# Second block's gated scan: the running maxima of all steps ahead of the scan, latent steps overlapped, two weightings on ScalarE, rows spread by a broadcast stationary operand

## The reference

```python
b = jnp.cumsum(lfc, axis=-1)
logd = jnp.where(mask, b[..., :, None] - b[..., None, :] + lic[..., None, :], -jnp.inf)
inter = b + m[..., None]
m_s = jnp.maximum(inter, jnp.max(logd, axis=-1))
dmat = jnp.exp(logd - m_s[..., None])
s = jnp.einsum('bhsd,bhrd->bhsr', qc, kc) * dmat
w_inter = jnp.exp(inter - m_s)
num = jnp.einsum('bhsr,bhrd->bhsd', s, vc) + w_inter[..., None] * jnp.einsum('bhvk,bhsk->bhsv', C, qc)
den = jnp.sum(s, axis=-1) + w_inter * jnp.einsum('bhk,bhsk->bhs', n, qc)
h = num / jnp.maximum(jnp.abs(den), jnp.exp(-m_s))[..., None]
log_w = b[..., -1:] - b + lic
m_new = jnp.maximum(b[..., -1] + m, jnp.max(log_w, axis=-1))
w = jnp.exp(log_w - m_new[..., None])
decay = jnp.exp(b[..., -1] + m - m_new)
C_new = decay[..., None, None] * C + jnp.einsum('bhr,bhrv,bhrk->bhvk', w, vc, kc)
```

## Time and profile before

| | us |
|---|---|
| median of 3 runs (4122.18 to 4126.77) | 4125.26 |
| the profiled execution | 4122.54 |
| its span in the trace | 4120.8 |
| first constant's DMA of the stage issued | at 2356.07 |
| last state update of the scan over | at 2546.65 |
| first DMA of the next stage issued | at 2691.06 |

### The profile page before, as it was taken

How to read it: one execution, slowest core, us unless ns; L and a number is a source line. 1 busy time by engine, 2 the same in 40 slices (tenths; PEclk the granted TensorE clock), 3 DMA queues, 4 the chain that set the end, 5 groups by cost and what they waited for, 6 DMA issues and landing times. The chain is left out here.

```text
span 4120.8 us, 37527 instructions
## 1 busy us (share of the span) xinstructions
PE 3426.4 (83%) x11876; PEld 1539.3 (37%) x11877; DVE 1973.6 (48%) x4086; ACT 659.6 (16%) x1532; POOL 932.9 (23%) x811
## 2 busy tenths in 40 slices
PE   7988998587899979999869845778788788888876
PEld 3345443332233323333335434544333233333332
DVE  5834223422333232232244055656666767667676
ACT  1011121000000000000022111412222222222212
POOL 2000000102222221021220040003444444444443
PEclk9999999699999989999989966899999999999998
DMA  9825333469999995597972000038999999999997
GB/s 333 284 87 200 137 115 114 188 229 408 376 364 366 364 412 233 215 363 283 385 262 98 27 0 0 1 150 345 421 415 412 421 408 408 422 403 422 417 421 327
DMA packets 194149, 1157.36 MB, mean 281 GB/s; under 512 B 25659, under 2 KB 27995, under 8 KB 74356
## 3 DMA queue, kind: packets, MB, share of 16 engines
q1 hardware_dynamic: 97140, 565.17, 35.3%
q0 software_dynamic: 80576, 564.05, 33.5%
q10 hardware_dynamic: 16320, 26.75, 2.1%
HBM read 1128.96 MB, written 48.68 MB: 286 GB/s over the span
## 5 line engine op out<-in xcount | busy, mean ns | idle before, releaser
L2462 DVE SCALAR_TENSOR_TENSOR mod<-q_uv,mix 128x1024 f32<-128x1024 f32 x512 | 627.1, 1225 | 391.5 <-DMA q_uv<-in_peer_uv,q_picks 387.0
L1149 PE MATMUL ps<-wt,e_xT 128*64 128x512 f32 x3200 | 729.4, 609 | 97.7 <-DMA wt<-in_w_exp 96.9
L2167 POOL DMA_INDIRECT q_uv<-in_peer_uv,q_picks x512 | 569.5, 1112 | 1053.9 <-PE ps L2259 720.8
L2259 PE MATMUL ps<-q_uv,q_dg 128*128 128x512 f32 x1024 | 518.7, 663 | 144.5 <-ACT q_dg L2336 144.5
L2259 PE MATMUL ps<-q_uv,tri 128*128 128x512 f32 x1024 | 465.4, 608 | 81.3 <-ACT tri L2336 81.3
L1129 POOL COPY wt<-e_land 128x2048 f32<-128x2048 f32 x124 | 237.7, 1917 | 1019.4 <-DMA e_land<-in_w_exp 1019.4
L1149 PEld LDWEIGHTS ps<-wt,e_xT 128*64 128x64 f32 x3200 | 236.9, 140 | 580.5 <-issue 430.0
L2259 PEld LDWEIGHTS ps<-q_uv,q_dg 128*128 128x128 f32 x1024 | 213.1, 213 | 441.1 <-issue 441.1
L1149 PE MATMUL ps<-wt,e_aT 128*64 128x512 f32 x1600 | 356.0, 597 | 21.5 <-ACT e_aT L1202 21.5
L2259 PEld LDWEIGHTS ps<-q_uv,tri 128*128 128x128 f32 x1024 | 194.9, 194 | 348.0 <-issue 347.9
L454 PE MATMUL ps<-hT,wt 128*128 128x512 f32 x640 | 285.1, 602 | 1.5 <-DVE wt L781 1.5
(11 more groups left out here) (439 smaller groups left out, 3402.7 us busy)
## 6 DMA issues: line engine op xcount, KB each, us to landing
wt<-in_w_exp SPq DMA_DIRECT2D x260, 1024.0 KB, 17.5
e_land<-in_w_exp SPq DMA_DIRECT2D x124, 1024.0 KB, 24.4
wt<-in_w_in_units SPq DMA_DIRECT2D x15, 2048.0 KB, 11.1
mod<-in_w_mod_units SPq DMA_DIRECT2D x48, 512.0 KB, 5.8
scratch_xs<-const_zeros SPq DMA_DIRECT2D x8, 2080.0 KB, 9.4
mod<-in_w_ada_units SPq DMA_DIRECT2D x32, 512.0 KB, 7.5
p_ring<-in_w_in SPq DMA_DIRECT2D x7, 2048.0 KB, 10.6
e_xg<-scratch_xs ACTq DMA_DIRECT2D x104, 128.0 KB, 7.3
```

What stands on the lines that cost most here:

```text
L1149: ins = nc.tensor.matmul(ps[64 * h:64 * h + 64, at, :], lhs[:, k % 4, 64 * (k // 4):64 * (k // 4) + 64], wt[:, u, a, h * W:(h + 1) * W], s ...
L2167: pool.indirect_dma_start(out=uv[:, n % NR, :, :].rearrange("p a d -> p (a d)"), out_offset=None, in_=A["peer_uv"], in_offset=bass.Indirec ...
L2259: last = nc.tensor.matmul(acc(t)[:, c, :], dg(n), uv[:, n % NR, 1, c * W:(c + 1) * W], start=fresh, stop=closing)
L2462: dve.scalar_tensor_tensor(junk[:, n % 2, :], uv[:, n % NR, 0, :], 1.0, mix[:, tile_of(k), :], ALU.mult, ALU.mult, accum_out=ap[:, k % 2, ...
```

## The change

It leaves GpSimd's work, the attention and every other stage as they were. In the scan:

- SyncE loads the gates' bias first, with a semaphore of its own (`s_bg`), and VectorE waits for it alone. The gate arrays are laid out direction first, so that the prefix sums take 3 products instead of 18.
- The sum of squares for the attention comes ahead of the scan.
- A first phase computes spreads and maxima for all six steps into arrays with an entry for each step (`mx`, `mr`, `ms`, `ek`, `eq`). A row is spread by using a column of `aa`, read with step 0 as a 128 x 128 stationary operand, against the identity (`spreads`), in banks 2 and 3 or 0 and 1 by turns. The logs of the latent steps are kept, one in `lgd` and three in the memory of `sq` (`logs`). The two context steps' states are made between the spreads. A second phase runs the four latent steps.
- ScalarE weights the keys (`weighted`, 8 instructions instead of VectorE's 2) and scales the state's product (8 instead of VectorE's 8). The first state is copied, not added to zeros, and the last one isn't made. `kw` has two buffers, in the memory of `qT`.
- TensorE's order in a latent step is: state's product, transposes, weighted keys by values, decayed products by values, then the next step's query-key products. VectorE divides a step's output after it has prepared the next one, and takes the statistics (`bn_stats`) as outputs become final.

```diff
@@ TensorE
+                def spreads(i):
+                    if i >= 2:
+                        pe.wait_ge(s_ar, i - 1)
+                    for u in range(8):
+                        last = nc.tensor.matmul(spread(i)[:, u // 4, (u % 4) * P:(u % 4 + 1) * P],
+                                                aa[:, i, u:u + 1].broadcast_to([P, P]), ident[:, :], start=True, stop=True)
+                    last.then_inc(s_ab, 1)
...
+                def states(i):
+                    pe.wait_ge(s_kw, i + 1)
+                    for u, (d, hh) in enumerate(units()):
+                        last = nc.tensor.matmul(sums_at(u, 5), kw[:, i % 2, u, :], va[:, steps[i][d], hh, :], start=True, stop=True)
+                    last.then_inc(s_kv, 1)
...
+                pe.wait_ge(s_aa, 1)
+                spreads(0)
+                spreads(1)
+                spreads(2)
+                states(0)
+                spreads(3)
+                pe.wait_ge(s_C, 1)
+                states(1)
+                spreads(4)
+                spreads(5)
+                pe.wait_ge(s_ar, NSTEP)
+                products(NTC)
+                for i in range(NTC, NSTEP):
+                    c = i - NTC
+                    pe.wait_ge(s_C, i)
+                    for u, (d, hh) in enumerate(units()):
+                        t = steps[i][d]
+                        last = nc.tensor.matmul(sums_at(u, 5), ct[:, hh, t * P:(t + 1) * P], CT[:, u, :], start=True, stop=True)
+                    last.then_inc(s_nm, 1)
+                    pe.wait_ge(s_s, c + 1)
+                    for u in range(8):
+                        last = nc.tensor.transpose(ps[:, u // 4, (u % 4) * P:(u % 4 + 1) * P], logs(c)[:, u, :], ident[:, :])
+                    last.then_inc(s_st, 1)
+                    if i + 1 < NSTEP:
+                        pe.wait_ge(s_ns, c + 1)
+                        states(i)
+                    pe.wait_ge(s_sT, c + 1)
+                    if c >= 1:
+                        pe.wait_ge(s_na, c)
+                    for u, (d, hh) in enumerate(units()):
+                        last = nc.tensor.matmul(sums_at(u, 2), sT[:, u, :], va[:, steps[i][d], hh, :], start=True, stop=True)
+                    last.then_inc(s_nm, 1)
+                    if i + 1 < NSTEP:
+                        products(i + 1)
@@ ScalarE
+                def weighted(i):
+                    if i >= 2:
+                        act.wait_ge(s_kv, i - 1)
+                    for u, (d, hh) in enumerate(units()):
+                        last = act.activation(kw[:, i % 2, u, :], kt[:, steps[i][d], hh, :], ACT.Copy, scale=ek[:, 0, i, u:u + 1])
+                    last.then_inc(s_kw, 1)
...
+                for c in range(NT):
+                    i = NTC + c
+                    act.wait_ge(s_nm, 2 * c + 1)
+                    if c >= 2:
+                        act.wait_ge(s_fin, c - 1)
+                    for u in range(8):
+                        last = act.activation(num[:, c % 2, u, :], sums_at(u, 5), ACT.Copy, scale=wsc[:, c, u:u + 1])
+                    last.then_inc(s_ns, 1)
+                    act.wait_ge(s_st, c + 1)
+                    act.copy(sT[:, :, :].rearrange("p (a b) s -> p a (b s)", a=2), ps[:, 0:2, :]).then_inc(s_sT, 1)
+                    if c + 1 < NT:
+                        decays(c + 1)
+                    if i + 2 < NSTEP:
+                        weighted(i + 1)
@@ VectorE
-                dve.wait_ge(s_load, 16 * 6)
+                dve.wait_ge(s_bg, 16)
...
+                for i in range(NSTEP):
+                    c = i - NTC
+                    dve.wait_ge(s_ab, i + 1)
+                    aB = spread(i).rearrange("p a (b r) -> p (a b) r", b=4)
+                    last = dve.tensor_reduce(mx[:, i, :], aB, AX_X, ALU.max)
+                    if c >= 0:
+                        for d in range(2):
+                            last = dve.tensor_tensor(logs(c)[:, 4 * d:4 * d + 4, :], aB[:, 4 * d:4 * d + 4, :],
+                                                     negm[:, d, :].unsqueeze(1).broadcast_to([P, 4, P]), ALU.add)
+                    last.then_inc(s_ar, 1)
...
+                decayed(0)
+                for c in range(NT):
+                    i = NTC + c
+                    if i + 1 < NSTEP:
+                        dve.wait_ge(s_xk, 2)
+                        state(i)
+                    dve.wait_ge(s_ns, c + 1)
+                    dve.wait_ge(s_nm, 2 * c + 2)
+                    for b in range(3):
+                        at, src = three(2, b)
+                        last = dve.tensor_tensor(num[:, c % 2, at, :], num[:, c % 2, at, :], src, ALU.add)
+                    last.then_inc(s_na, 1)
+                    if c + 1 < NT:
+                        decayed(c + 1)
+                    outcome(c)
```

More of the change, by code:

```diff
@@ L1719, in _ @@
             def _(pe):
[L1721 to L1727, removed]
@@ L1763, in _ @@
+                pe.wait_ge(s_na, NT)
                 pe.wait_ge(s_qk, 1)
@@ new lines, in decays @@
+                def decays(c):
+                    for u in range(8):
+                        last = act.activation(logs(c)[:, u, :], logs(c)[:, u, :], ACT.Exp, bias=nbias[:, c, u:u + 1])
+                    last.then_inc(s_d, 1)
+                act.wait_ge(s_rq, 1)
+                act.activation(rq[:, :, :], rq[:, :, :], ACT.Sqrt).then_inc(s_sd, 1)
+                act.wait_ge(s_ek, 1)
+                act.activation(ek[:, :, 0:NTC, :], ek[:, :, 0:NTC, :], ACT.Exp).then_inc(s_xk, 1)
+                act.wait_ge(s_xk, 1)
@@ new lines, in _, with state @@
+                link(last)
+                for i0, t0, n in ((0, NT, NTC), (NTC, 0, NT)):
+                    dve.tensor_tensor(aa[:, i0:i0 + n, 0:4], gv[:, t0:t0 + n, 0, 0, :], ab[:, i0:i0 + n, 0, 0:4], ALU.subtract)
+                for i in range(NSTEP):
+                    last = dve.tensor_tensor(aa[:, i, 4:8], gv[:, steps[i][1], 1, 0, :], ab[:, i, 0, 4:8], ALU.subtract)
+                last.then_inc(s_aa, 1)
+                dve.wait_ge(s_aa, 1)
+                def state(i):
+                    dve.wait_ge(s_kv, i + 1)
+                    if i == 0:
+                        for b in range(3):
+                            at, src = three(5, b)
+                            last = dve.tensor_copy(CT[:, at, :], src)
+                    else:
+                        dve.wait_ge(s_C, i)
+                        for u in range(8):
+                            last = dve.scalar_tensor_tensor(CT[:, u, :], CT[:, u, :], ek[:, 1, i, u:u + 1], sums_at(u, 5), ALU.mult, ALU.add)
+                    last.then_inc(s_C, 1)
@@ L1977, in _ @@
-                    if i == 1:
-                        dve.wait_ge(s_sd, 1)
-                        dve.reciprocal(rq[:, :, :], rq[:, :, :]).then_inc(s_rr, 1)
-                for t in range(NT):
-                    for hh in range(MH):
-                        last = dve.bn_stats(st[:, t, hh, :], hm[:, t, hh * MD:(hh + 1) * MD])
-                link(last)
+                        for t in tiles:
+                            for hh in range(MH):
+                                last = dve.bn_stats(st[:, t, hh, :], hm[:, t, hh * MD:(hh + 1) * MD])
```

249 lines of the change are left out of this document (114 added, 135 removed).

## The result

The changed kernel takes 4031.47 us, median of 4 runs (4027.39 to 4037.19); the kernel before, on the same chip, 4126.02 (4122.18 to 4127.24). The ratio is 0.9773 (95% interval 0.9756 to 0.9790). Forecast were 4042 and a range of 4029 to 4066: right in direction and range, 10.5 us too slow in size.

The account below looks back on a forecast made before the run. Engines wait for each other, TensorE and VectorE alternating in the scan. Terms laid on the old clock moved the attention's start from 2546.65 to 2463.4: 83 us off 4122.54, 4039.5, plus 2.7 for the median: 4042, range 4029 to 4066.

Parts of the forecast that it names:

- That the whole gain reaches the end: Scan: whatever it saves up to 2546.65 should reach the kernel's end, 83 us, unless the attention runs otherwise.
- Early load at nothing, addition held by GpSimd: Stage start: GpSimd's work seems to hold the bias's addition, so the earlier load counts nothing, at most 2.8 us.
- First phase 39.4: Scan's first phase: spreads, maxima, masks and context states from 2371.9 to 2411.3, 39.4 us.
- The run-in: Between the phases: last maximum, exponents, decays, weightings and first scaling, from 2411.3 to 2421.6.
- the signs: What would show it: first maxima at about 2372, next DMA stage about 2608, circle 10 to 12 us, among others.
- The circle, 10.4: Latent step: state's product, ScalarE's scaling 2.5, three more products at 1.95 each and hand-overs, 10.4 us; three circles 31.2.
- Both on VectorE would bound the circle: Latent step: scaling on VectorE would shorten the circle by 0.3, but VectorE's 10.6 us of work would bound it.
- Allowances, 2 for GpSimd and 4 for the clock: Second phase: 2 us for GpSimd's work beside VectorE's, 4 us for half of one circle's doubling at the lower clock.
- The low clock: Rival, second phase: it stays at the 1.2 GHz level, circle 17.8, 20 us more, 4062; chance 0.2.
- Slow step-0 loads: Rival, spreads: one-column loads cost extra, 4061 or even 4130; chance of slower 0.01, of 4050 to 4061 0.07.
- The order rival: Rival, latent steps: VectorE's in-order list holds TensorE up, circle 2 to 3 us longer, 4050; no chance given.
- The giving back in the attention: Rival, attention: half of sixteen pairs fall to the lower clock, giving back 15 us, 4057; chance 0.07.

Follow-up runs that it names:

- e9: The changed kernel with GpSimd's squares started only when the gate columns are ready and their sum behind the third step's maxima; 4024.9 us in one profile.
- e4: The changed kernel with the keys' weighting and the scaling of the state's product both back on VectorE; 4039.5 us in one profile.
- e2: The changed kernel with only the scaling of the state's product back on VectorE; 4029.6 us in one profile.
- e1: The changed kernel with the latent steps taken one after the other again; 4061.42 us, median of 4, ratio 0.9846.
- e5: The changed kernel with spreads made as before, two 512-column products of ones against diagonals built by VectorE; 4039.3 us in one profile.

## Why the prediction was right, step by step

*That the whole gain reaches the end.* Right within the scatter. The scan lost 91.9 us and the next stage's first DMA comes 91.4 earlier; that the two agree so closely is chance, since the stage began 4.7 us later and the attention was 4.2 shorter.

*Early load at nothing, addition held by GpSimd.* Right, and now shown: 4.21 us beside the squares, ending with them, and 0.26 in e9 without them. By the rule of the Trainium skill's page "SBUF — State Buffer", section "SBUF: two separate sides", this is a lock; the runs agree, in that the instruction beside GpSimd stood until GpSimd's ended. First spread forecast 15.8 us behind the first DMA, measured 15.3.

*First phase 39.4.* Measured 36.9: 0.7 less up to the first keys product, 0.8 up to the second (the spread between them took 1.95, where 2.9 was taken, while the product itself took 3.4 and not 2.9), and 1.0 up to the last mask, where VectorE's pieces begin before the end of the one ahead (a maximum of 1.23 at 2404.20, its mask at 2405.35) and the 0.5 for GpSimd was not needed. The run-in was 9.8, not 10.3. (One sum is 0.1 too large: 2401.7 + 4.2 + 2.16 is 2408.1. And among the signs the first maxima stand at about 2372, which in the sum itself is the first spread; on the old clock the first maximum came at 2375.6.)

*The circle, 10.4.* Measured 9.7, three times 0.7 less; only the first phase was missed by more. The path was the right one, with TensorE's wait on ScalarE's scaling. Mis-sized was the scaling, 2.5 for 2.18: the nearest row was L1835, which reads SBUF. The four products came to 7.45 (1.88, 1.79, 1.79 and 1.99 between the starts of one and the next, the last up to the scaling) and not 7.8, because each starts before the modelled end of the one ahead. 0.3 and 0.35, and 0.05 of hand-over, make the 0.7.

*Both on VectorE would bound the circle.* Right in direction, 11.0 us in e4, but not by VectorE's load, forecast at 10.6 us: it had 8.13 in the first circle, and the place of the weighting in its list accounts for the rest. On VectorE the scaling doesn't shorten the circle by 0.3 either, 9.75 and 9.72 in e2, since it costs 2.17 there and 2.18 on ScalarE.

*Allowances, 2 for GpSimd and 4 for the clock.* From the first keys product (2422.71) to the attention (2459.49) it was 36.8 us, where the prediction had 31.2 + 4.6 + 6 = 41.8. Of the 5.0 between them 2.1 are the three circles, 2.0 the allowance for GpSimd, of which nothing shows there, 0.7 the clock, and 0.2 the last step. The clock took 3.3: 1.7 in a first circle of 11.3, 1.7 in a last product of 3.62. In the second profile of the same kernel it took 1.1 (circle 9.7, last product 3.07). GpSimd's work on queries and keys took 45.5 us, not 50.7, and ended at 2425.2 on the old clock, not near 2432.

*Outside the scan.* Not forecast: attention 4.2 less, the stages around it 6.7 more. Both lie in what one kernel does from run to run: the changed kernel's attention took 140.2 and 144.4, and its stage's first DMA came at 2360.72 and 2355.34. So they show no effect of the change. The scan's misses sum to 0.5 + 2.5 + 0.5 + 5.0 = 8.5 us, the 2.6 outside stand against them: 89.3 us were saved instead of 83. Nearly every term of the scan was set too long, so its fit is not one of large errors that cancel. The other 4.5 of the 10.5 come from the medians: it lies 1.8 under the profiled execution, where 2.7 above it had been added.

*Rivals.* The low clock did not come: 0.91 over the second phase. In e1, with the steps in a row, it was 0.68. That e1's 4061 lies near the rival's 4062 is chance: its circle is 20.6 with waits in it, the rival's was 17.8 at the lower price throughout. Slow step-0 loads are refuted by the 1.95 of the changed kernel's own spread and by e5. The order rival is refuted by the wait of 1.4 on ScalarE; e4 shows what it looks like, 2.75 on VectorE. The giving back in the attention did not come: it took 140.2 and 144.4, against 144.4 before.

## What to carry to other kernels

Where engines alternate on a serial chain, take out of it first what does not depend on the carried state, and then let the next step's products start before this one's output is finished: here the second part was worth 11 us a circle, half of it waits and half the granted clock that came back with them. Before moving work to another engine, look at what stands between two links of the chain in that engine's list: each of the two weightings was free on either engine, but both in a row on VectorE cost the circle the second one's length. When an early input gains nothing, look at what runs beside its consumer: here moving GpSimd's squares brought the first gate 4.0 us forward, which the earlier load could not.

## What the runs showed of the hardware that was not expected

- A matrix operand read with step 0 (one column spread to 128) costs TensorE what any other does: 16 entries in 1.95 us at the upper clock, as four dense ones of 512 columns in 1.96.
- ScalarE's copy with a factor for each partition is quicker out of PSUM than out of SBUF: eight of 129 columns in 2.18 us out of PSUM, eight of 128 in 2.43 to 2.46 out of SBUF.
- One kernel's scan took 98.8 and 95.3 us in two profiles, by where the granted clock falls; small edits of this kind are judged by marks ahead of the first such place, or by many runs.
